# The second feed-forward products of a two-block transformer kernel, written as seven products of quarters

## The reference

```python
D_MODEL = 1024; SEQ = 512; D_FF = 4 * D_MODEL
D_FF_2 = -(-8 * D_MODEL // (3 * 256)) * 256          # 2816

# first block
h = rms_norm(x, g_mlp[l])
x = x + jnp.square(jax.nn.relu(h @ w_ff1[l])) @ w_ff2[l]
# ...
# second block
hn = rms_norm_2(h, ffn_norm_g[l])
h = h + (jax.nn.silu(hn @ w_ffn_gate[l]) * (hn @ w_ffn_up[l])) @ w_ffn_down[l]
```

## Time and profile before

| what | value |
|---|---|
| time, three runs | 1561.93, 1564.98, 1571.24 us; median 1564.98 us |
| span of the profiled execution (first to last instruction) | 1563.8 us, 1.2 us less than the median |
| matmul busy (PE), weight load busy (PEld) | 1523.4 us, 1216.0 us |
| VectorE, ScalarE, GpSimd busy | 823.6, 615.0, 349.0 us |
| mean granted TensorE clock | 0.991 of full speed |
| HBM read, written | 142.78 MB, 9.55 MB |

### The profile page before, as it was taken

How to read it: one execution, slowest core, us unless ns; L and a number is a source line. 1 busy time by engine, 2 the same in 40 slices (tenths; PEclk the granted TensorE clock), 3 DMA queues, 4 the chain that set the end, 5 groups by cost and what they waited for, 6 DMA issues and landing times.

```text
span 1563.8 us, 19842 instructions
## 1 busy us (share of the span) xinstructions
PE 1523.4 (97%) x7330; PEld 1216.0 (78%) x7330; DVE 823.6 (53%) x1673; ACT 615.0 (39%) x1123; POOL 349.0 (22%) x367
## 2 busy tenths in 40 slices
PE   7999989999999999999999999999999999999997
PEld 5786656788888888888888778766688888888887
DVE  5556676344455343433446787587374543443444
ACT  6433577322244232322446433566444322222232
POOL 3300445100020000000036634445442110120112
PEclk9999999999999999999999999999999999999999
DMA  5763100423233223323322663312332333322231
GB/s 195 139 156 107 50 15 1 147 95 95 82 108 94 94 95 95 95 95 102 100 89 68 159 161 114 115 48 82 135 95 82 107 95 98 104 95 95 95 95 55
DMA packets 47838, 154.13 MB, mean 99 GB/s; under 512 B 5842, under 2 KB 8082, under 8 KB 47744
## 3 DMA queue, kind: packets, MB, share of 16 engines
q1 hardware_dynamic: 43008, 137.63, 27.7%
q0 software_dynamic: 4736, 15.25, 4.6%
HBM read 142.78 MB, written 9.55 MB: 97 GB/s over the span
## 4 chain that ended last, share of the span: by engine, by line
PE 87%; DVE 6%; ACT 3%; issue 2%; DMA 2%; SPq 0%; POOL 0%; DVEq 0%; ACTq 0%
PE PSA L608 85%; PE PSA L835 2%; DMA WR<-w_in 1%; PE PSA L979 1%; DVE WL L1793 1%; DMA XT<-xT_in 0%; ACT AR L1385 0%; DVE AR L1907 0%; DVE AHL L2000 0%; ACT AHL L1434 0%; DVE Al L1793 0%; ACT WH L1316 0%; ACT Ah L1316 0%; DVE AR L2000 0%; DVE AR L2252 0%
## 5 line engine op out<-in xcount | busy, mean ns | idle before, releaser
L608 PE MATMUL PSA<-Ah,WH 128*128 128x512 f32 x1072 | 424.3, 396 | 11.3 <-DVE Al L1801 8.6
L608 PE MATMUL PSA<-Al,WH 128*128 128x512 f32 x1072 | 419.7, 392 | 0.0
L608 PE MATMUL PSA<-Ah,WL 128*128 128x512 f32 x1072 | 419.7, 391 | 0.0
L1316 ACT CAST WH<-WR 128x1024 fp32r<-128x1024 f32 (+3 forms) x229 | 236.9, 1036 | 230.0 <-PE PSA L608 216.8
L1793 DVE TENSOR_TENSOR WL<-WR,WH 128x1024 fp32r<-128x1024 f32 (+3 forms) x202 | 250.7, 1241 | 86.7 <-ACT WH L1316 86.4
L608 PEld LDWEIGHTS PSA<-Ah,WH 128*128 128x128 f32 x1072 | 202.9, 189 | 60.3 <-issue 17.6
L608 PEld LDWEIGHTS PSA<-Ah,WL 128*128 128x128 f32 x1072 | 202.8, 189 | 42.9
L608 PEld LDWEIGHTS PSA<-Al,WH 128*128 128x128 f32 x1072 | 202.9, 189 | 42.2 <-issue 0.7
L608 PE MATMUL PSA<-Bh,WH 128*128 128x512 f32 (+2 forms) x580 | 221.9, 383 | 4.6 <-DVE Bl L2071 2.3
L608 PE MATMUL PSA<-Bh,WL 128*128 128x512 f32 (+2 forms) x580 | 220.3, 380 | 0.0
L608 PE MATMUL PSA<-Bl,WH 128*128 128x512 f32 (+2 forms) x572 | 217.7, 381 | 0.0
(11 more groups left out here) (378 smaller groups left out, 2029.6 us busy)
## 6 DMA issues: line engine op xcount, KB each, us to landing
WR<-w_in SPq DMA_DIRECT2D x228, 512.0 KB, 3.6
gt_tmp<-AR SPq DMA_DIRECT2D x16, 256.0 KB, 2.1
WR<-w_in SPq DMA_DIRECT2D x8, 384.0 KB, 3.1
XT<-scr_tmp POOLq DMA_DIRECT2D x8, 264.0 KB, 13.7
XT<-scr_tmp POOLq DMA_DIRECT2D x8, 256.0 KB, 14.3
XT<-xT_in POOLq DMA_DIRECT2D x1, 2048.0 KB, 9.2
x_tmp<-XT POOLq DMA_DIRECT2D x1, 2048.0 KB, 7.7
AHL<-gt_tmp SPq DMA_DIRECT2D x8, 256.0 KB, 3.9
```

The costliest lines, as they stand in the source:

```text
L608: return pe.matmul(o, l, r, start=start, stop=stop)
L1316: ac.copy(halves(j)[0][:, 0:n], WR[j % RAW][:, 0:n]).then_inc(w_hi, 1)
```

## The change

All of the first part's groups but the last half of the fourth, and the first two groups of the second part, make their output tiles in another way. Four output tiles (a "sub", 512 output features) by eight hidden tiles by 512 tokens are taken as a product of 2x2 quarters and made with seven products of quarters in place of eight (a form of Strassen's algorithm, with sums that build on each other). There are seven such subs in the first part and four in the second.

- The tokens are halved (columns 0:256 and 256:512), the hidden tiles are paired (even and odd), the output features of a sub are halved. A product of quarters is 4 hidden tiles x 2 output tiles x 3 matmuls = 24 matmuls of 128x256. A sub has 7 x 24 = 168 of them in place of 4 x 24 = 96 of 128x512.
- Weights: a sub still loads four tiles of 128x1024, now the four quarters. Four sums of them are made by VectorE on 128x1024 (`weight_sum`: s3, s1, s2, s4). The seven products use the quarters a11, a12, a22 and the sums s1 to s4 as stationary operands, each cast and subtracted as before: 7 casts and 7 subtractions per sub in place of 4. The quarter a21 goes into sums only.
- Activations: of each pair of hidden tiles VectorE makes four sums of 128x256 (`pair_sums`), ScalarE casts them together as 128x1024 (`sums_high`), VectorE subtracts (`sums_low`). Both subs of a group use them. `Bh` and `Bl` of even tiles are needed, and made, for the first 256 tokens only.
- Results: eight additions to `XT` of 128x2x256 per sub in place of four of 128x512; some products add to a bank that has been read already.
- Places in the queue of VectorE: in the first part the subtraction of the split tile, a `sums_low` and a weight sum now stand ahead of the wait for TensorE's result.

The core of the diff (the second part and the bookkeeping are cut):

```diff
+PRODUCTS = ("a11", "a12", "s1", "s2", "a22", "s3", "s4")
+SUMS = ("s3", "s1", "s2", "s4")
+SUBS1 = [(q, s) for q in range(4) for s in range(2)][:7]
+SUBS2 = [(c, s) for c in range(2) for s in range(2)]
...
+        SUM_AT = {(0, 4): "s3", (0, 6): "s1", (1, 0): "s2", (1, 2): "s4"}
...  TensorE
+                def multiply(what, rows, o, start):
+                    wh, wl = halves_ready(product(u, what))
+                    for c in range(4):
+                        xh, xl = rows(c)
+                        for e in range(2):
+                            c0, oo = 256 * c + 128 * e, o[:, 256 * e:256 * e + 256]
+                            a, b = wh[:, c0:c0 + 128], wl[:, c0:c0 + 128]
+                            first = start and c == 0 and e == 0
+                            pe.matmul(oo, a, xh, start=first, stop=False, skip_group_check=True)
+                            pe.matmul(oo, a, xl, start=False, stop=False, skip_group_check=True)
+                            last = pe.matmul(oo, b, xh, start=False, stop=c == 3, skip_group_check=True)
+                    last.then_inc(w_mm, 1)
...
+                multiply("a11", quarter(even, 0), XB, True)
+                multiply("a12", quarter(odd, 0), ZB, True)
+                if s:
+                    pe.wait_ge(added, in_sub(ph, g, 0, 8))
+                multiply("s1", summed(0), YB, True)
+                pe.wait_ge(added, in_sub(ph, g, s, 1))
+                multiply("s2", summed(1), XB, False)
+                multiply("a22", summed(3), WB, True)
+                pe.wait_ge(added, in_sub(ph, g, s, 4))
+                multiply("s3", summed(2), XB, False)
+                pe.wait_ge(added, in_sub(ph, g, s, 3))
+                multiply("s4", quarter(odd, 256), YB, False)
...  ScalarE, first part
+                    if i in (2, 4, 6):
+                        sums_high(1, q, i // 2 - 1)
...
-                    ac.activation(Bh[:, i, :], RT[s], ACT.Square).then_inc(f_hi, 1)
+                    w = T if i % 2 or (q, 1) not in SUBS1 else 256
+                    ac.activation(Bh[:, i, 0:w], RT[s][:, 0:w], ACT.Square).then_inc(f_hi, 1)
...  VectorE
+            def weight_sum(u, what):
...
+                if what == "s3":
+                    dv.tensor_tensor(b3, tile(l11), tile(l21), ALU.subtract).then_inc(w_sum, 1)
+                elif what == "s1":
+                    dv.tensor_tensor(b1, tile(l21), tile(l22), ALU.add).then_inc(w_sum, 1)
+                elif what == "s2":
+                    dv.wait_ge(w_sum, sum_no(u, "s3"))
+                    dv.tensor_tensor(b2, tile(l22), b3, ALU.subtract).then_inc(w_sum, 1)
+                else:
+                    dv.wait_ge(w_sum, sum_no(u, "s2"))
+                    dv.tensor_tensor(b4, tile(l12), b2, ALU.subtract).then_inc(w_sum, 1)
...
+            def pair_sums(ph, g, p, h0, h1):
...
+                dv.tensor_tensor(t3, h1[:, 256:512], h0[:, 256:512], ALU.subtract).then_inc(y_t, 1)
+                dv.tensor_tensor(t1, h0[:, 256:512], h0[:, 0:256], ALU.subtract).then_inc(y_t, 1)
+                dv.wait_ge(y_t, 4 * n + 1)
+                dv.tensor_tensor(t2, h0[:, 0:256], t3, ALU.add).then_inc(y_t, 1)
+                dv.wait_ge(y_t, 4 * n + 3)
+                dv.tensor_tensor(t4, h1[:, 0:256], t2, ALU.subtract).then_inc(y_t, 1)
...
+                for k, what in enumerate(PRODUCTS):
+                    split_to(tid["sw", 7 * u + k] + 2)
+                    if s == 0 and k == 0:
+                        sums_low(ph, g, 3)
+                    if (g, 1) in (SUBS1 if ph == 1 else SUBS2) and (s, k) in SUM_AT:
+                        weight_sum(sub_of(ph, g, 1), SUM_AT[s, k])
+                    result(product(u, what))
+                    if what == "a11":
+                        gather(XB, 0, 0, 0)
...  VectorE, first part
+                    if n > 1:
+                        split_to(tid["f1", n] + 2)
+                    if i in (2, 4, 6):
+                        sums_low(1, q, i // 2 - 1)
+                    if i > 3:
+                        weight_sum(sub_of(1, q, 0), SUMS[i - 4])
                     result(tid["f1", n])
...
-                    if n > 1:
-                        split_to(tid["f1", n] + 2)
                     dv.wait_ge(f_hi, n + 1)
-                    dv.tensor_tensor(Bl[:, i, :], RT[s + 1], Bh[:, i, :].bitcast(F), ALU.subtract).then_inc(f_lo, 1)
+                    w = T if i % 2 or (q, 1) not in SUBS1 else 256
+                    dv.tensor_tensor(Bl[:, i, 0:w], RT[s + 1][:, 0:w], Bh[:, i, 0:w].bitcast(F), ALU.subtract).then_inc(f_lo, 1)
+                    if i % 2:
+                        pair_sums(1, q, i // 2, RT[2 * ((n - 1) % 4) + 1], RT[s + 1])
```

More of the change, by code:

```diff
@@ L30 @@
 SIZES2 = (8, 8, 6)
+PRODUCTS = ("a11", "a12", "s1", "s2", "a22", "s3", "s4")
+QUARTERS = ("a11", "a21", "a22", "a12")
+SUMS = ("s3", "s1", "s2", "s4")
+SUBS1 = [(q, s) for q in range(4) for s in range(2)][:7]
+SUBS2 = [(c, s) for c in range(2) for s in range(2)]
 X_LOADS = (0, 1), (1, 1), (2, 2), (4, 2), (6, 2)
@@ L66, in tile_list, with load_list @@
             t += [("fg", f + i, 1024, True), ("fu", f + i, 1024, True)]
-        t += [("fd", 8 * c + i, n * 128, True) for i in range(8)]
+        t += [("sw", 7 * (len(SUBS1) + u) + i, 1024, True) for u, (p, s) in enumerate(SUBS2) if p == c for i in range(7)]
+        t += [("fd", 8 * c + i, n * 128, True) for i in range(8) if (c, i // 4) not in SUBS2]
         f += n
     return t
+def load_list(tiles):
+    out = []
+    for j, (name, i, n, split) in enumerate(tiles):
+        if name != "sw":
+            out.append((name, i, n, j))
+        elif i % 7 == 0:
+            out += [("sw", 4 * (i // 7) + b, n, None) for b in range(4)]
+    return out
 class Sig:
@@ L109, in build, with load_of @@
                 lo_no[j] = n_lo_
+    def load_of(j):
+        name, i = tiles[j][0:2]
+        if name != "sw":
+            return lid[name, i]
+        what = PRODUCTS[i % 7]
+        return lid["sw", 4 * (i // 7) + QUARTERS.index(what)] if what in QUARTERS else None
     with ExitStack() as ctx:
@@ L155, in bank, with raw, halved @@
             return PSA[:, i, :]
+        def raw(l):
+            return WR[l % RAW]
+        def halved(j):
+            name, i, n = tiles[j][0:3]
+            l = load_of(j)
+            if l is None:
+                return SUMB[i // 7 >= len(SUBS1)][SUMS.index(PRODUCTS[i % 7])], [X.rearrange("p (a c) -> p a c", a=4) for X in halves(j)]
+            return raw(l)[:, 0:n], [X[:, 0:n] for X in halves(j)]
         ident = CST[:, 0:128]
@@ L592, in sync_program @@
                      tid["wo2", 2]: (12, 13), tid["wo2", 3]: (14, 15)}
-            for j in range(2, len(tiles)):
+            for l in range(2, len(loads)):
+                j = loads[l][3]
                 if j in out_at:
@@ L1830, in scaled, with tile @@
                 dv.tensor_tensor(P, P, rb, ALU.mult).then_inc(e_z.sem, 1)
+            def weight_sum(u, what):
+                l11, l21, l22, l12 = (lid["sw", 4 * u + b] for b in range(4))
+                b3, b1, b2, b4 = SUMB[u >= len(SUBS1)]
+                def tile(l):
+                    dv.wait_ge(w_ld[l % RAW], 16 * (l // RAW + 1))
+                    return raw(l)[:, :].rearrange("p (a c) -> p a c", a=4)
+                if u not in (0, len(SUBS1)):
+                    dv.wait_ge(w_lo, lo_no[product(u - 1, what)])
+                if what == "s3":
[5 more added lines that the diff above has]
+                    dv.tensor_tensor(b2, tile(l22), b3, ALU.subtract).then_inc(w_sum, 1)
+                else:
+                    dv.wait_ge(w_sum, sum_no(u, "s2"))
+                    dv.tensor_tensor(b4, tile(l12), b2, ALU.subtract).then_inc(w_sum, 1)
```

322 lines of the change are left out of this document (236 added, 86 removed).

## The result

The changed kernel takes 1580.51 us (median of four runs, 1576.47 to 1585.20), the kernel before 1564.55 us (the three runs of the table and a fourth, 1564.12). The ratio is 1.0094, 95% interval 1.0067 to 1.0121: slower by about 1%, where 1567 us was forecast and 1552 to 1578 was the range. The profiled execution of after took 1578.5 us with a span of 1576.7, 12.9 us longer than that of before.

A forecast was written before the change was run, and what follows sets the result against it. TensorE's matmuls were taken to bound the kernel, with VectorE's queue becoming late in the first part. -17.6 + 8.4 + 9.2 + 0.4 + 1.5 = +1.9 us on a 1563.8 us span gave a 1567 us median, range 1552 to 1578.

The forecast's parts named there:

- seven products of 0.1200 us matmuls: TensorE, 11 subs: 168 matmuls at 0.1200 us replace 96 at 0.2267, saving 1.60 us per sub, 17.6 us in all.
- group one: late queue 9.2 and clock 1.5: First part, first group: TensorE waits for late VectorE work lose 9.2 us, one slow-clock stretch behind them 1.5 us.
- groups two to four: `Bl` and split of s1: First part: TensorE waits for late `Bl` in a12 and s1's split, 2.8 us per group, 8.4 us in three.
- clock in groups two and three: First part: no slow-clock stretch expected behind these groups' waits, so 0 us.
- second part's waits: Second feed-forward part: VectorE's added work makes TensorE lose 0.4 us over two groups.
- the walk of VectorE's queue: Instruction-by-instruction timing of VectorE's queue: a tile pair costs it 12.35 us of TensorE's 10.88, so relus come late.
- Some 0.2 us lost in each of two groups: Second part: tile 7's late multiply and s1's nearly late split cost TensorE 0.2 us per group, 0.4 us together.
- The other groups' gaps are 0.9 and 1.9 us with work between; I take none: First part, groups two to four: TensorE's waits are taken to bring no slow-clock stretch, so no clock loss.
- Rival C: The clock falls in every group of the first part, 3 x 1.5 us more, 1571.5 us; chance 0.14.
- A: Rival: VectorE keeps up, added instructions fill its gaps and TensorE hardly waits, 1548 us; chance 0.13.
- B: Rival: tiles 3 to 7, dependent VectorE instructions don't overlap, each costing its duration plus 0.03 us; 1580 us; chance 0.18.

The follow-up runs named there:

- ReLU first: Changed kernel reordered only: first part's ReLU leads VectorE's queue, ScalarE squares earlier, s4 among products, second part's sums moved, two small edits; 1550.66 us, ratio 0.9905 to before.
- after's second execution: The changed kernel profiled once more with no edit, to see how much a stage differs by itself; 1576.06 us, span 1574.3.

## Why the prediction was wrong

By its own steps. Measured are stages of after (first profile) less those of ReLU first, which has almost no waits; the waits of groups two and three are taken from after's second execution, at full clock, and what the first one has above them is the clock:

| step | forecast | measured |
|---|---|---|
| seven products of 0.1200 us matmuls | -17.6 | -17.6 (six stages of ReLU first less before) |
| group one: late queue 9.2 and clock 1.5 | +10.7 | +10.7 (1.02 + 49.96 - 40.32) |
| groups two to four: `Bl` and split of s1 | +8.4 | +10.15 (2.89, 2.90 and 4.36) |
| clock in groups two and three | 0 | +2.8 (0 in the second execution) |
| second part's waits | +0.4 | +2.4 |
| untouched stretches | 0 | +4.5 |
| sum | +1.9 | +12.9 |

The steps make 11 us of the 13.5 between 1567 and the measured 1580.51 us; the profiled execution was 2 us faster than the median.

- **The gain and the walk of VectorE's queue were right.** The pace was forecast to 0.001 us. Of groups two and three the waits were 0.86 and 1.9 us by the walk and 0.88 and 1.77 by the trace; of group one 2.2, 1.0, 1.5 and 3.5 by the walk and 2.1, 0.9, 1.5 and 3.4 in the second execution. The undoing of one cause, the sums ahead of the ReLU, took the waits of groups two and three away entirely.
- **Failed: "Some 0.2 us lost in each of two groups".** The walk charged 1.14 us for each sum, wherever it stood. s1's stands beside GpSimd's 2.21 us and pays 1.1 us more: 1.2 us per group. (`sums_low` pays it one tile earlier, where 2.45 us of idle take it up.) The order without that meeting loses nothing.
- **Failed: "The other groups' gaps are 0.9 and 1.9 us with work between; I take none".** The clock fell behind 8 of 16 gaps of 1.77 us; it cost 1.4 us in each of after's groups two and three, and 2.5 in group four of its second execution. Rival C had the mechanism, as a thing that comes in every group or in none; it comes in some.
- **Missed: group four.** The walk has `Bh` and `Bl` of even tiles at half width in every group, and "The change" says so too; in this one they are made for all 512 tokens, as its second half is unchanged. Tile 7's ReLU begins 3.61 us behind the stage's start and not 3.18 as in group two, the wait for `Bl` was 1.3 and not 0.9 us, and the unchanged half waits 0.94 us for the last addition of the half ahead of it, a wait for all eight that the forecast didn't go through. Together 1.5 us.
- **Untouched stretches.** The middle holds slow stretches that lose 1.2 to 3.6 us each: two and three in the executions of before, four in after, in twelve executions of changed kernels one to six; its length is 384.5 to 392.4 us. Less what they lose (3.2 us in before, 6.2 in after, by the distances between matmul starts), it is 383.0 us in both and 380 to 384 us in all fourteen. So the 3.0 us are the clock by execution, not work that the change added; whether changed kernels meet on the average more of these stretches stays open, as before was profiled only twice. The start of the first part lies at 464.4 to 472.4 us in the same executions, so its 1.5 us say nothing either. The four timed runs of after stand in the order of their granted clocks: 1576.47 us at 0.987, 1578.50 at 0.983, 1582.53 at 0.982, 1585.20 at 0.978.
- **Rivals.** A was refuted as told and is what ReLU first reached (1550.66 against its 1548): VectorE can keep up, not in the order of the change. B named 1580, nearly the time, for a wrong reason: the four pair sums stand 0.34, 0.34 and 0.45 us apart (594.05 to 595.18 in after), as walked, where B wanted 0.45 each, and 128x1024 stand 1.14 apart, not 1.25. A hit of its time is no sign for it.
- **The range** took 0.5 us per group for what wasn't seen, and nothing for the clock in stretches that the change doesn't touch, though the runs of before alone spread over 9 us (1561.93 to 1571.24).

## What to carry to other kernels

Before work goes into the queue of a half-idle engine, look at where its idle time lies: here 1.0 to 1.2 us behind each ReLU, waiting for ScalarE, would hold a sum for nothing, while the same sum ahead of the ReLU delays all that hangs on it. The consumer's result comes first in the queue, what has a late deadline goes into the wait behind it; 25 to 27 us lie between the spans of after and of ReLU first (1576.7 and 1574.3 against 1549.6), which issue the same instructions in another order. And keep instructions with two SBUF inputs on VectorE away from GpSimd's, and a saving near 1% out of places where TensorE would then stand still.
